# All 22 units of the gate and up projection by seven block products, in two passes over the weights

## The reference

```
FFN_HIDDEN = ((8 * D_MODEL + 767) // 768) * 256
def swiglu_ffn(h, w_in, w_out):
    gate, up = jnp.split(h @ w_in, 2, axis=-1)
    return (jax.nn.silu(gate) * up) @ w_out
...
        h = rms_norm_2(x, pre2_w[l]) * (1.0 + sc2) + sh2
        y = swiglu_ffn(h, ffn_w_in[l], ffn_w_out[l])
        x = x + (1.0 + gt2) * rms_norm_2(y, post2_w[l])
```

## Time and profile before

| | us |
|---|---|
| device time, median of 3 runs (2195.97 to 2196.33) | 2195.98 |
| the profiled execution, its own time | 2195.21 |
| span of its profile | 2193.5 |
| TensorE busy in the span | 2156.8 (98%) |
| seven-product units, 1631.07 to 1936.00 | 304.9 |

### The profile page before, as it was taken

How to read it: one execution, slowest core, us unless ns; L and a number is a source line. 1 busy time by engine, 2 the same in 40 slices (tenths; PEclk the granted TensorE clock), 3 DMA queues, 4 the chain that set the end, 5 groups by cost and what they waited for, 6 DMA issues and landing times.

```text
span 2193.5 us, 29234 instructions
## 1 busy us (share of the span) xinstructions
PE 2156.8 (98%) x11168; PEld 1754.8 (80%) x11168; DVE 1125.7 (51%) x1371; ACT 701.6 (32%) x874; POOL 1156.3 (53%) x1080
## 2 busy tenths in 40 slices
PE   7999999999999999999999999999999999999997
PEld 5788887887777877787888888887878888888886
DVE  7988874357543261361497236655743333335207
ACT  6663342335433232112122331234323333212112
POOL 3342224566652332222584344566677777767776
PEclk9999999999999999999999999999999999999999
DMA  6224414232421111112233334432532222345343
GB/s 229 90 106 173 171 56 148 77 105 87 154 83 43 58 49 61 55 49 78 87 125 107 106 133 144 162 119 86 195 111 86 86 76 77 120 159 183 134 154 125
DMA packets 84256, 243.70 MB, mean 111 GB/s; under 512 B 7616, under 2 KB 18112, under 8 KB 84160
## 3 DMA queue, kind: packets, MB, share of 16 engines
q1 hardware_dynamic: 71808, 223.51, 28.8%
q10 hardware_dynamic: 12352, 18.88, 2.3%
HBM read 203.03 MB, written 39.32 MB: 110 GB/s over the span
## 4 chain that ended last, share of the span: by engine, by line
PE 89%; DVE 5%; ACT 2%; DVEq 1%; POOLq 1%; DMA 1%; issue 1%; POOL 0%; ACTq 0%; SPq 0%
PE PG L810 39%; PE PG L816 19%; PE PG L1371 14%; PE PG L1311 6%; PE PX L810 2%; PE PX L816 1%; PE PX L1040 1%; DVE PX L2218 1%; PE PX L1035 1%; PE PG L911 1%; DVE WK L2212 1%; PE PX L1018 1%; PE PX L1055 1%; PE PX L988 0%; PE PX L1283 0%
## 5 line engine op out<-in xcount | busy, mean ns | idle before, releaser
L810 PE MATMUL PG<-UL,WH 128*128 128x512 f32 x1712 | 668.1, 390 | 0.0
L810 PE MATMUL PG<-UH,WH 128*128 128x512 f32 x1584 | 632.2, 399 | 5.0 <-DVE UL L2223 1.6
L687 POOL TENSOR_TENSOR TOUCH<-TOUCH 128x2 f32<-128x2 f32 x186 | 56.2, 302 | 831.6 <-PE PG L816 697.4
L690 POOL TENSOR_TENSOR WL<-WRAW,WH 128x1024 fp32r<-128x1024 f32 (+1 forms) x186 | 439.9, 2365 | 30.5 <-issue 30.5
L816 PE MATMUL PG<-UH,WL 128*128 128x512 f32 x1584 | 404.9, 390 | 0.0
L810 PEld LDWEIGHTS PG<-UL,WH 128*128 128x128 f32 x1712 | 321.9, 188 | 68.0 <-issue 4.1
L810 PEld LDWEIGHTS PG<-UH,WH 128*128 128x128 f32 x1584 | 297.4, 188 | 82.6 <-issue 11.9
L816 PEld LDWEIGHTS PG<-UH,WL 128*128 128x128 f32 x1584 | 297.4, 188 | 62.2
L688 POOL TENSOR_SCALAR WH<-WRAW 128x1024 fp32r<-128x1024 f32 (+1 forms) x186 | 191.6, 1030 | 0.0
L751 POOL TENSOR_TENSOR W2L<-W2RAW,W2H 128x1024 fp32r<-128x1024 f32 (+1 forms) x48 | 114.4, 2383 | 7.9 <-issue 7.7
L1371 PE MATMUL PG<-TH,AL 128*128 128x512 f32 x256 | 99.7, 389 | 0.0
(11 more groups left out here) (597 smaller groups left out, 3883.2 us busy)
## 6 DMA issues: line engine op xcount, KB each, us to landing
ADA<-ada_w SPq DMA_DIRECT2D x24, 1024.0 KB, 5.1
W2RAW<-down_w SPq DMA_DIRECT2D x48, 512.0 KB, 3.3
RAW<-up_w SPq DMA_DIRECT2D x16, 1024.0 KB, 4.8
WRAW<-out_w SPq DMA_DIRECT2D x30, 512.0 KB, 3.2
WRAW<-zg_w SPq DMA_DIRECT2D x24, 512.0 KB, 3.2
gates<-STG ACTq DMA_DIRECT2D x24, 512.0 KB, 2.6
WK<-gates SPq DMA_DIRECT2D x24, 512.0 KB, 3.3
WRAW<-up_w SPq DMA_DIRECT2D x24, 512.0 KB, 3.2
```

The lines of the kernel that those rows point to most:

```text
L687: pool.tensor_tensor(TOUCH[:, 0:2], TOUCH[:, 2:4], TOUCH[:, 4:6], ALU.add)
L690: pool.tensor_tensor(WL[:, r, 0:n], WRAW[:, r, 0:n], WH[:, r, 0:n].bitcast(F32), ALU.subtract).then_inc(w_split, 1)
L810: mm = pe.matmul(out, w[:, r, at + P * k:at + P * k + P], v, start=first and k == ks[0] and n == 0, stop=False)
```

## The change

All 22 units go by seven products, and these are cut in two passes:

- **Gate pass** (stage gate_up, 22 tiles). Only the gate weights are loaded (gate_pair, 512 KB a unit, split by split_tile). TensorE makes P1 in one bank of PG and A12 B21 in the next (gate_unit, 24 matmuls); both need only the first half of the tokens. ScalarE copies P1 into PGB, VectorE adds it to the other bank (gate_join), ScalarE takes silu of that sum (gate_value). Both results go to DRAM as one 128x1024 row (p1_out, 512 KB), and all of it is read again in the second pass (p1_in). The work on the second half of the tokens, h_save and t_blocks, cut in three parts, stands between the units of this pass.
- **Second pass.** 22 units of five products (S2, S3, S1, A22, S4: 60 matmuls). The weights of a unit, gate and up, are loaded whole (raw_in). P1 and the first gate come from DRAM, so first_copy, gate_first and the high and low parts of A11 and A12 are gone.
- The first half of units 0 to 5 is no longer in SBUF: it is read back during unit 16 (hidden_in, 6 units in one DMA) and split among units 16 to 21.

```diff
@@ SyncE
+            for i in range(11):
+                gate_pair(i)
+                for n in (2 * i - 4, 2 * i - 3) if i >= 2 else ():
+                    p1_out(n)
+                if i == 4:
+                    sp.wait_ge(h_made, 2 * KB)
+                    for j in range(KB):
+                        sp.dma_start(h_save[j * P:(j + 1) * P, :], H[:, j, :]).then_inc(h_saved, 16)
...
+            def unit_moves(i, p, first=False):
+                sp.wait_ge(a_low, i * 5 + (LOW0 + A22 + 1))
                 raw_in(i + 2, p)
+                if not first:
+                    value_out(1, i - 1, 1 - p)
                 value_out(0, i, p)
+                p1_in(i + 2, p)
...
+            unit_moves(15, 1)
+            sp.wait_ge(values_saved[0], SAVED0 + 32 * 8)
+            sp.wait_ge(values_saved[1], SAVED0 + 32 * 7 + 16)
+            hidden_in(0, 0, 6, UHF[:, 0:6, 0:512], 4)
+            hidden_in(0, 6, 4, UHF[:, 0:4, 512:1024], 0)
+            unit_moves(16, 0)
@@ GpSimd, unit_weights
+                pool.wait_ge(raw_loaded[p], i * 8 + (RAW_LOADED0 + 16 - 8 * p))
+                pool.tensor_tensor(S1_RAW[:], a21(p), a22(p), ALU.add)
                 pool.drain()
+                pool.wait_ge(a_used, i * 5 + (USED0 - 5 + S2 + 1))
+                pool.tensor_tensor(SUMS[:, S2, :], S1_RAW[:], RAW[p][:, 0, 0:512], ALU.subtract).then_inc(sums_made, 1)
                 pool.drain()
+                pool.tensor_tensor(S4_RAW[:], RAW[p][:, 0, 512:1024], SUMS[:, S2, :], ALU.subtract).then_inc(sums_made, 1)
+                pool.wait_ge(a_used, i * 5 + (USED0 - 5 + S3 + 1))
+                pool.tensor_tensor(SUMS[:, S3, :], RAW[p][:, 0, 0:512], a21(p), ALU.subtract).then_inc(sums_made, 1)
                 pool.drain()
+                for w, of in ((S2, SUMS[:, S2, :]), (S3, SUMS[:, S3, :]), (S1, S1_RAW[:]), (A22, a22(p)), (S4, S4_RAW[:])):
+                    pool.wait_ge(a_high, i * 5 + (HIGH0 + w + 1))
+                    pool.tensor_tensor(AL[:, w, :], of, AH[:, w, :].bitcast(F32), ALU.subtract).then_inc(a_low, 1)
@@ TensorE
+            def gate_unit(n, r):
+                pe.wait_ge(ffn_silu, n - 1)
+                pe.wait_ge(w_high, n + (TILE0["gate_up"] + 1))
+                gate_products(r, 0, KB, False)
+                pe.wait_ge(w_split, n + (TILE0["gate_up"] + 1))
+                gate_products(r, 0, KB, True).then_inc(tile_done, 1)
+
+            for r, k0, k1 in ((0, 0, 6), (1, 0, 6), (0, 6, KB), (1, 6, KB)):
+                if k0 == 0:
+                    pe.wait_ge(slot_free[r], UNIT0["down0"] // 2)
...
+            pe.wait_ge(ffn_silu, N_HIDDEN)
             with pe.Fori(0, UNITS) as i:
                 pe.wait_ge(norm_lo, 80)
+                block_product(i, S2, PG[:, 0, :], t_block(2))
+                pe.wait_ge(joined, i * 6 + (JOINED0 - 1))
+                block_product(i, S3, PG[:, 1, :], t_block(3))
+                block_product(i, S1, PG[:, 2, :], t_block(1))
+                pe.wait_ge(joined, i * 6 + (JOINED0 + 2))
+                block_product(i, A22, PG[:, 1, :], t_block(4))
                 block_product(i, S4, PG[:, 3, :], b_block(4, 1))
@@ ScalarE
+            def gate_value(n):
+                act.wait_ge(tile_done, TILE0["gate_up"] + n + 1)
+                if n >= 2:
+                    act.wait_ge(values_saved[n % 2], P1_SAVED0 + 16 * (n // 2))
+                act.activation(PGB[:, n % 2, 0:512], PG[:, 2 * (n % 2), :], ACT.Copy).then_inc(p1_copied, 1)
+                act.wait_ge(joined, GATE_JOINED0 + n + 1)
+                act.activation(PGB[:, n % 2, 512:1024], PG[:, 2 * (n % 2) + 1, :], ACT.Silu).then_inc(ffn_silu, 1)
...
+            for n in range(11, 21):
+                gate_value(n)
+                for k, part in T_PARTS[n]:
+                    t_high(k, part)
...
+            def unit(i, p):
+
+                high_last(i)
+                gate_second(i - 1)
+                unit_highs(i + 1, 1 - p)
+
+            unit_highs(0, 0, True)
+            gate_value(21)
...
+            unit(15, 1)
+            act.wait_ge(hidden_loaded[4], LOADED0[4] + 16)
+            for i in range(16, UNITS - 1):
+                unit(i, i % 2)
+                split_hidden(0, i - 16)
@@ VectorE
+            u2_blocks(0, 0, 8)
+            for u in range(2, 4):
+                post_add(1, u)
...
+            for n in range(11, 21):
+                gate_join(n)
+                for k, part in T_PARTS[n]:
+                    t_blocks(k, part)
+            gate_join(21)
+            with dve.Fori(0, 8) as i:
                 for p in range(2):
                     join_unit(i * 2 + p, p)
+            for i in range(16, UNITS):
+                join_unit(i, i % 2)
+                split_low(0, i - 16)
```

More of the change, by code:

```diff
@@ L579, in _ @@
+            for p in range(2):
+                sp.wait_ge(values_saved[p], P1_SAVED0 + 16 * 9)
+            for p in range(2):
+                p1_in(p, p)
+            p1_out(18)
+            p1_out(19)
             sp.wait_ge(w_split, TILE0["down0"])
             raw_in(1, 1)
[L581 to L585, removed]
+            p1_out(20)
+            p1_out(21)
+            for p in range(2):
+                sp.wait_ge(values_saved[p], SAVED0)
@@ new lines, in _, with unit_highs @@
+            half_root2(11)
+            for n, j0, j1 in ((8, 0, 3), (9, 3, 6), (10, 6, 8)):
+                gate_value(n)
+                for j in range(j0, j1):
+                    u2_high(1, j)
+            for n in range(11, 21):
+                gate_value(n)
+                for k, part in T_PARTS[n]:
+                    t_high(k, part)
+            def high(w, of):
+                act.activation(AH[:, w, :], of, ACT.Copy).then_inc(a_high, 1)
+            def unit_highs(i, p, first=False):
+                act.wait_ge(sums_made, i * 3 + (SUMS0 + 1))
+                high(S2, SUMS[:, S2, :])
+                act.wait_ge(sums_made, i * 3 + (SUMS0 + 3))
+                high(S3, SUMS[:, S3, :])
+                for w, of in ((S1, S1_RAW[:]), (A22, a22(p))):
+                    if not first:
+                        act.wait_ge(a_used, i * 5 + (USED0 - 5 + w + 1))
+                    high(w, of)
@@ L2097, in gate_first @@
-            def gate_first(i):
-                act.wait_ge(joined, i * 7 + (JOINED0 + 5))
-                act.activation(WK[:, 18, half_tok(0)], PX[:, 3, :], ACT.Silu).then_inc(ffn_silu, 1)
-            def unit(i, p, first=False, last=False):
-                high_last(i, first)
-                if not first:
-                    gate_second(i - 1)
-                first_copy(i)
-                if not last:
-                    high_first(i + 1, 1 - p)
-                    high_sum(i + 1, S2)
-                gate_first(i)
-                if not last:
-                    for w in (S3, S1):
-                        high_sum(i + 1, w)
-                    for w in (A12, A22):
-                        high_raw(i + 1, 1 - p, w)
@@ L2117, in _ @@
-            high_first(0, 0, True)
-            for w in (S2, S3, S1):
-                high_sum(0, w)
-            gate_value(1, 5)
-            for w in (A12, A22):
-                high_raw(0, 0, w, True)
-            unit(0, 0, first=True)
-            with act.Fori(0, UNITS // 2 - 1) as i:
+                act.wait_ge(joined, i * 6 + (JOINED0 + 6))
+                act.activation(G1[:], PX[:, 2, :], ACT.Silu).then_inc(ffn_silu, 1)
+            def unit(i, p):
+                high_last(i)
+                gate_second(i - 1)
+                unit_highs(i + 1, 1 - p)
@@ L3170, in _ @@
+            for u in range(2, 4):
+                post_add(1, u)
+            for n in range(2):
+                gate_join(n)
+            dve.wait_ge(norm_rs, 11)
+            for n, us in ((2, (0,)), (3, (1, 2)), (4, (3,))):
+                gate_join(n)
+                for u in us:
+                    residual(1, u)
+            gate_join(5)
+            for u in range(1, 3):
                 pre_add(1, u)
-            hidden_value(0, 3)
+            gate_join(6)
+            pre_add(1, 3)
@@ L3172, in _ @@
+            gate_join(7)
             dve.wait_ge(norm_rs, 12)
[L3173 to L3185 removed]
```

468 lines of the change are left out of this document (188 added, 280 removed), and 4 rows, old and new, of tables (SOURCE, STREAM).

## The result

| | before | changed |
|---|---|---|
| median, 4 runs of each on one chip (us) | 2196.15 (2195.97 to 2197.06) | 2205.31 (2202.16 to 2208.74) |
| profiled execution, its own time | 2195.21 | 2202.16 |
| its span | 2193.5 | 2200.4 |

The ratio is 1.0041, interval 1.0028 to 1.0053: slower by 0.4%, where 2193.1 and "within 0.2%" had been forecast. Two things stand out: the changed kernel is slower although it has 72 matmuls less, and its runs lie 6.6 us apart, those of before 1.1.

What follows compares the result with a forecast made beforehand. PE, busy 98%, was taken as the bound, 0.2269 us a matmul. 72 fewer matmuls (-16.3) and the start (-0.4), against waits of +0.5, +1.9, +1.5, +2.7, 0, +4.5, +2.7, gave -2.9: 2193.1 us, range 2186 to 2200.

Steps and rivals of the forecast that it cites:

- 2 start: Start of gate pass: two old PE waits go (-2.0), tile 1 waits for banks out2_unit frees (+1.6); together -0.4 us.
- 3 gate pass: Gate pass: copy, join and silu fit under a unit's 5.44 us; only half_sum before unit 8 costs PE; +0.5 us.
- 4 h_save: Gate pass: copy of unit 8 waits for p1_out(6), issued behind h_save; +1.9 us, from 0 to 4.
- 5 sums T: Late gate pass: late join 14 and t_blocks make PE wait before units 18 to 21; +1.5 us, 0 to 5.
- 6 into second pass: Start of second pass: PE waits for all 22 silus, 4.5 us against 1.8 before; +2.7 us, 0.5 to 4.
- 7 loop: Second-pass units: GpSimd's 12.2 us, DVE, ACT and transfers stay hidden under PE's 13.61 us; 0 us.
- 8 hidden units: Second pass, unit 16: ACT waits for the hidden-units read, so U3 reaches product A22 late; +4.5 us, 3 to 7.
- 9 out of it: Before the first down tile: last split_low stands behind join_unit(21), 3.2 us after the last matmul; +2.7 us, 2.4 to 3.2.
- clock: Rival: clock falls in gaps of 4.5, 4.5 and 3.2 us, two or three times 1.6 us; 2196 to 2198; chance 0.15.
- late P1 rows: Rival, gate pass: nine even units each wait 1.3 us for p1_out of two units before; +12, 2205 us; chance 0.10.
- part of the waits don't come: Rival: early p1_out landings or a faster 1.5 MB hidden-units read shrink the forecast waits; 2184 to 2191 us; chance 0.28.
- POOL becomes the bound: Rival, second-pass loop: POOL operations take 1.70 us, above about 1.4, a unit 16 us; +50 us; chance 0.05.

Runs made afterwards that it cites:

- Experiment 1: Changed kernel with each saved row issued right behind the load of the tile four units later, not in pairs: 2196.61 us, ratio 1.0002.
- Experiment 8: Changed kernel saving only the P1 half of each row (256 KB), read twice, first gate's silu left out, same issue order: 2204.15 us, ratio 1.004.
- experiments 5: Changed kernel with saved rows issued singly, hidden-units wait behind unit 16, last hidden split one unit earlier, last-silu wait moved to S1: 2180.47 us, ratio 0.993.
- 7: Kernel of experiments 5 with tile 0 made whole before tile 1 and h_save issued 3, 2, 3 behind tiles 9 to 11: 2177.84 us, ratio 0.9914.
- 11: The kernel of experiment 7 unchanged, run again on another chip: 2176.33 us.
- experiment 2: Changed kernel with ScalarE's wait for the hidden units moved from before unit 16 to behind it: 2199.87 us, ratio 1.0016.
- kernel 10: Kernel of experiment 7 with ScalarE's wait for the hidden units put back before unit 16: 2184.09 us, 7.8 over kernel 11.

## Why the prediction was wrong, point by point

Against the profiled execution before, +6.95 us was measured (2202.16 less 2195.21), and -2.9 forecast. By its steps:

| step | forecast | measured | from |
|---|---|---|---|
| 1 matmuls | -16.3 | -16.3 | spacing 0.227 wherever nothing was late |
| 2 start | -0.4 | -0.5 | slot wait cost 1.4, not 1.6; the two of before 1.9 |
| 3 gate pass | +0.5 | +4.5 | unit 4 1.9, norm sum 2.6 |
| 4 h_save | +1.9 | +1.9 | unit 10, 1.8 and the handover |
| 5 sums T | +1.5 | +2.0 | 0.8, 0.4, 0.7 before units 14, 18, 20 |
| 6 into second pass | +2.7 | +2.0 | 3.75 against 1.8 |
| 7 loop | 0 | 0 | first 218.6 us of it: busy 218.56 |
| 8 hidden units | +4.5 | +4.8 | 4.64 and the handover |
| 9 out of it | +2.7 | +2.9 | 3.31 from start to start, less 0.23 and 0.15 |
| clock | 0 | +4.8 | 1.7, 1.5, 1.6 behind three gaps |
| rest | | +0.9 | pieces too small to name |

**The step that failed first is 3**, "no PE cost here", through a price that stands in step 5: the saved row "lands 3.0 to 3.7 later". It took 5.1. The issue was forecast right: for unit 2 at 1511.2 by the formula, and it came at 1511.8. With 3.4 us it would have landed 2.8 us after TensorE finished unit 2; the rival "late P1 rows" gave +3.2 as the point from which that costs, and with 5.1 it is 4.6. So the mechanism was in the text with a chance of 0.10 and belonged in the sum; the prediction's own sign of being wrong, even gate units that wait for landings, came at seven of them. The rival's price was too high, 12 us for nine units, and that its 2205 is the measured median is luck: the rows cost some 8 us in the table above, and the clock, which the rival left out, 4.8.

Units 4, 8 and 10 lost time, 1.9, 2.6 and 1.9, and three later ones 2.0 together, and the second pass began 1.4 us later than the seven products before it, where the text had some 6 us earlier. What the text did not have is the detour by which unit 8 lost its 2.6: the late landing goes over the join into VectorE's order and holds up pre_add, and that the norm sum. Experiment 1 shows both: moving the save took away the 4.5 us of step 3, the 1.7 of the clock behind them, the 2.0 of step 5 (the text had a late join 14 and the sums T together there; with the rows in time the sums T alone make TensorE wait nowhere) and 0.9 of step 6, 9.1 of the 10.1 by which the second pass starts earlier.

Why the row of a tile load is the wrong measure: the earlier trace rows have writes of 256 KB (2.0) and reads of 512 KB (3.3) where the DMA share is 0.24; this one is a write behind reads at 0.58. Experiment 8 rules out the bytes as the main part; why the landing takes 5.1 and not 3.4, whether by the reads ahead of it or by its direction, stays open, since no run separates them.

**The second thing that failed is the chance of the clock** (0.15, on top of the sum). The profiles of nine kernels (all but those of before and of experiments 5, 7 and 11) have 23 gaps of 2.4 to 6.4 us in TensorE's stream after 1450 us, that at the very end left out. In or just behind 19 of them the granted clock falls to 0.50. In 18 of the 19 some 6 to 14 matmuls then start 0.42 apart, which costs 1.2 to 2.8 us; in the other (experiment 2, before the norm sum) the low clock falls on the matmuls of the norm sum. Of the gaps up to 2.2 us none did it, and between 1450 us and the last gap the clock is low nowhere else. Behind gaps of 3.8 us and more it was so in each of six; between, in 13 of 17, and the same gap of 3.6 before the second pass was followed by it in three kernels and not in the changed one. The rule that the prediction quoted (the Trainium skill, TensorE: Matmul & The Clock Gate, "Why this matters for your kernels": no idle gaps above about 3 us) is borne out in kind; the traces have the low clock already behind 2.5 and 2.9 us, and once not behind 3.6.

The clock also fits the spread, but that is argued and not shown, since only one execution of each kernel has a trace. The four runs of the changed kernel have granted clocks of 0.995, 0.995, 0.994 and 0.993 in the order of their times. The 0.002 between the first and the last is 4.4 us of 2207 (2 to 6.6 with the rounding), and the times are 6.6 apart. The profiled execution was the fastest one, so the table above may be some 3 us short of the median.

**What held.** Steps 8 and 9 and the slot wait came at the named instructions and within 0.3 us; 4 and 5 within 0.5, though 5 at other units than forecast, 6 within 0.7, and the loop of step 7 at nothing. Step 8 moves with the landing of the 1.5 MB: 7.2, 8.0 and 9.4 us in the traces of kernel 10, the changed kernel and kernel 1 gave waits of 3.9, 4.6 and 6.0. The rival "part of the waits don't come" was wrong throughout: all came. "POOL becomes the bound" was wrong too: the low parts take 1.30 us each in the changed kernel.

**Where the gain went.** 16.3 us of matmuls and 0.5 at the start were taken away and 23.8 put back: 18.1 in waits of the new order (steps 3 to 6, 8 and 9), 4.8 in the clock and 0.9 in pieces not named. None of the waits belongs to the idea. With all of them gone but 1.2 us, the same work takes 2177.84, and 2176.33 when run again: 18 to 20 us under the kernel before, more than the 16.3 of the forecast's first term. The 1.8 that TensorE waited at the start of the seven products before is part of the difference; so are the two waits of the earlier trace rows.

## What to carry to other kernels

When a buffer is freed by a save, walk the save's place in the queue to each reuse of the buffer, and price its landing from a row with the same direction and neighbours, or, where there is none, with some 1.5 times the nearest one (an estimate from this one case, 5.1 for 3.4); then check for every engine whether something on the critical path stands behind the instruction that waits. Price every new gap in TensorE's stream above some 2.4 us with 1.5 us more than its length, an estimate from the 23 gaps above. A change that removes work and comes out slower is to be read by its waits one by one before it is given up: here four edits of one to three lines each turned +9 us into -15, and two more into -18.

## What the runs showed of the hardware

- The low clock can begin late: behind a gap of 3.87 us the first three matmuls start 0.33, 0.23 and 0.23 apart and only then eight 0.42 apart (kernel 10). In kernel 1 the slow ones began 1.9 us after a gap of 2.9; in the changed kernel, behind 4.6, at the second matmul.
- Writing 256 KB instead of 512 KB behind the same loads shortened the landing from 5.1 to 4.4 us only.
- Eight issues of h_save took 8.8 us of SP before, 10.3 in the changed kernel, and 9.4 in kernel 1; what makes the difference was not tested.
